# A hybrid decoder layer on one core: first tiles of two feed-forward networks taken block by block, and index scores placed between projection matmuls

## The reference

```python
def _swiglu(x, wg, wu, wd):
    return (jax.nn.silu(x @ wg) * (x @ wu)) @ wd

def _indexer_topk(qi, wi, q_pos, ki, topk):
    s = jnp.einsum('bqhd,bld->bqhl', qi, ki).astype(jnp.float32) * (IDX_DIM ** -0.5)
    score = jnp.einsum('bqhl,bqh->bql', jax.nn.relu(s), wi.astype(jnp.float32)) * (IDX_HEADS ** -0.5)
    ...

def _macaron_layer(x, mixer, f1g, f1u, f1d, ln1g, ln1b, ln2g, ln2b, f2g, f2u, f2d, ln3g, ln3b):
    x = _layernorm(ALPHA * x + 0.5 * _swiglu(x, f1g, f1u, f1d), ln1g, ln1b)
    m, st = mixer(x)
    x = _layernorm(ALPHA * x + m, ln2g, ln2b)
    x = _layernorm(ALPHA * x + 0.5 * _swiglu(x, f2g, f2u, f2d), ln3g, ln3b)
    return x, st
```

## Time and profile before

| | us |
|---|---|
| median of three runs | 1435.36 (1432.1 to 1439.06) |
| the profiled execution | 1438.75 |
| its span in the trace | 1437.1 |
| PE busy | 1372.3 (95% of the span) |
| ACT busy | 451.1 |
| DVE busy | 552.1 |
| POOL busy | 184.6 |

### The profile page before, as it was taken

How to read it: one execution, slowest core, us unless ns; L and a number is a source line. 1 busy time by engine, 2 the same in 40 slices (tenths; PEclk the granted TensorE clock), 3 DMA queues, 4 the chain that set the end, 5 groups by cost and what they waited for, 6 DMA issues and landing times.

```text
span 1437.1 us, 26868 instructions
## 1 busy us (share of the span) xinstructions
PE 1372.3 (95%) x10066; PEld 1201.4 (84%) x10066; DVE 552.1 (38%) x1105; ACT 451.1 (31%) x694; POOL 184.6 (13%) x250
## 2 busy tenths in 40 slices
PE   6999999999999999999999989998899999999994
PEld 6999999999997656777766665567799999999994
DVE  3333233322234236899020444436433333332236
ACT  3343333322233231112231403324533333322234
POOL 0000000033422301222460030003100000000020
PEclk9999999999999989999999978999899999999997
DMA  4222222233322324788757666501132222223231
GB/s 173 88 88 82 80 86 88 84 89 106 106 78 97 120 66 143 260 268 259 265 191 224 222 217 217 191 16 44 44 88 88 88 88 88 88 70 88 88 92 63
DMA packets 69454, 176.78 MB, mean 123 GB/s; under 512 B 9681, under 2 KB 13778, under 8 KB 69138
## 3 DMA queue, kind: packets, MB, share of 16 engines
q1 hardware_dynamic: 59090, 148.09, 32.5%
q0 software_dynamic: 9440, 24.18, 5.1%
q10 hardware_dynamic: 864, 3.73, 0.7%
HBM read 168.93 MB, written 7.02 MB: 122 GB/s over the span
## 4 chain that ended last, share of the span: by engine, by line
PE 93%; DVE 3%; ACT 2%; DMA 1%; issue 1%; ACTq 0%; POOL 0%; DVEq 0%
PE ps L377 91%; PE ps L380 2%; DMA xbuf<-in_x_t 1%; ACT scr L915 1%; DVE scr L1293 1%; DVE rbuf L1286 0%; ACT xbuf L915 0%; ACT x_high L915 0%; DVE rbuf L1298 0%; DVE w_low L1203 0%; ACT big L915 0%; ACT lg L915 0%; ACT w_high L915 0%; DVE big L1286 0%; DVE scr L1276 0%
## 5 line engine op out<-in xcount | busy, mean ns | idle before, releaser
L377 PE MATMUL ps<-x_high,w_high 128*128 128x280 f32 (+1 forms) x1408 | 414.4, 294 | 23.8 <-DVE x_low L1209 10.3
L377 PE MATMUL ps<-x_high,w_low 128*128 128x280 f32 (+1 forms) x1408 | 412.3, 293 | 0.0
L377 PE MATMUL ps<-x_low,w_high 128*128 128x280 f32 (+1 forms) x1408 | 412.1, 293 | 0.0
L1203 DVE TENSOR_TENSOR w_low<-wring,w_high 128x1024 fp32r<-128x1024 f32 (+1 forms) x136 | 166.8, 1228 | 497.2 <-ACT w_high L915 497.1
L377 PEld LDWEIGHTS ps<-x_high,w_high 128*128 128x128 f32 x1408 | 269.2, 191 | 26.6 <-issue 20.0
L915 ACT ACTIVATE w_high<-wring 128x1024 fp32r<-128x1024 f32 (+1 forms) x136 | 140.5, 1034 | 413.1 <-PE ps L377 399.3
L377 PEld LDWEIGHTS ps<-x_low,w_high 128*128 128x128 f32 x1408 | 269.9, 192 | 0.0
L377 PEld LDWEIGHTS ps<-x_high,w_low 128*128 128x128 f32 x1408 | 269.3, 191 | 0.0
L377 PE MATMUL ps<-xbuf,wring 128*128 128x280 f32 x1056 | 263.6, 405 | 5.0 <-ACT xbuf L915 4.1
L377 PEld LDWEIGHTS ps<-xbuf,wring 128*128 128x128 f32 x1056 | 197.5, 191 | 59.6 <-issue 9.1
L377 PE MATMUL ps<-h_high,w_high 128*128 128x280 f32 (+1 forms) x704 | 204.5, 290 | 0.0
(11 more groups left out here) (201 smaller groups left out, 1175.3 us busy)
## 6 DMA issues: line engine op xcount, KB each, us to landing
dring<-in_v_pool SPq DMA_DIRECT2D x128, 256.0 KB, 3.5
wring<-in_wg SPq DMA_DIRECT2D x44, 512.0 KB, 3.5
wring<-in_wu SPq DMA_DIRECT2D x44, 512.0 KB, 3.5
wring<-in_w_in SPq DMA_DIRECT2D x33, 512.0 KB, 4.1
wring<-in_wd SPq DMA_DIRECT2D x32, 512.0 KB, 3.6
dring<-in_k_pool POOLq DMA_DIRECT2D x64, 256.0 KB, 4.4
dring<-in_k_pool SPq DMA_DIRECT2D x64, 256.0 KB, 3.8
wring<-in_wd SPq DMA_DIRECT2D x16, 384.0 KB, 3.1
```

The lines of the kernel that those rows point to most:

```text
L377: return nc.tensor.matmul(out, lhs, rhs, start=start, stop=stop, **kw)
L1203: v.tensor_tensor(wl[:, to, 0:n], w4[:, s, 0:n], wh[:, to, 0:n].bitcast(F32), ALU.subtract) \
```

## The change

**First network.** PE takes tile 0 block by block, both weights and both halves of a block together (12 matmuls), and then `tile(1)` as before. ACT and DVE split up 0 right after the first x block. The constants are issued behind ACT's x splits. SP waits for all four quarters of x before it issues the third and fourth weight tile.

**Second network.** A second pair of buffers (`wh2`, `wl2`, laid over memory that is idle then) takes the splits of gate 1 and up 1, made in the norm: ACT after the fourth square, DVE ahead of the last two adds. PE does half 0 of tiles 0 and 1 together block by block (12 matmuls a block), then half 1 weight by weight. `first_pair` on ACT and DVE handles the hidden values of both tiles and splits the weights of tile 2; the loops of ACT and DVE run one round less.

**Query tiles.** The transposes of the head weights stand between the halves of query tile 0. The scores of queries t stand between the products of query tile t: after each product of the second half for t = 0, after every other product for t = 1 to 3. ACT evicts the tile behind its eight Relus. What `index_queries` and `index_scores` hold was in line before and is unchanged.

```diff
+        w_high2, w_low2 = (over(f"w_{n}2", 2048, h_at + (ZT * T + 2048 * i) * 4) for i, n in enumerate(("high", "low")))
...
                     f, up = divmod(s, 2)
+                    if m == 0 and s == 2:
+                        for q in range(4):
+                            sp.wait_ge(sem(f"xw_in{q}"), 16)
                     weight(s, (wus if up else wgs)[m][f], first=(m == 0))
...
-            def wide_split(m, p, s, high, low, k0=0, kn=KT, total=KT, parts=(0, 1), ready=None, ks=None):
+            def wide_split(m, p, s, high, low, k0=0, kn=KT, total=KT, parts=(0, 1), ks=None, hi=wh, lo=wl):
 
                 for a in parts:
                     for k in ks or range(kn):
-                        if ready is not None:
-                            pe.wait_ge(sem("xl_done"), ready + k + 1)
-                        for j, (w_, x_) in enumerate(((wh, high), (wh, low), (wl, high))):
+                        for j, (w_, x_) in enumerate(((hi, high), (hi, low), (lo, high))):
...
                 pe.wait_ge(sem("h_done"), hdone.up())
-                for a in range(2 if m else 0):
-                    if a == 0:
-                        pe.wait_ge(sem("wl_done"), wl_done.up(2))
+                if m == 0:
                     for k in range(KT):
-                        pe.wait_ge(sem("xl_done"), KT * (1 + a) + k + 1)
+                        pe.wait_ge(sem("xl_done"), k + 1)
                         for up in range(2):
-                            last = wide_split(1, 2 * up, up, xh, xl, parts=(a,), ks=(k,))
-                            if a and k == KT - 1:
+                            if k == 0:
+                                pe.wait_ge(sem("wl_done"), wl_done.up())
+                            last = wide_split(0, 2 * up, up, xh, xl, ks=(k,))
+                            if k == KT - 1:
                                 last.then_inc(sem(f"w_free{up}"), 1)
-                for a in range(0 if m else 2):
-                    for up in range(2):
-                        if a == 0:
-                            pe.wait_ge(sem("wl_done"), wl_done.up())
-                        last = wide_split(m, 2 * up, up, xh, xl, parts=(a,),
-                                          ready=None if up or a > m else KT * (m + a))
-                        if a:
-                            last.then_inc(sem(f"w_free{up}"), 1)
-                tile(1)
+                    tile(1)
+                else:
+                    pe.wait_ge(sem("h_done"), hdone.up())
+                    pe.wait_ge(sem("wl_done"), wl_done.up(4))
+                    split = [dict(), dict(hi=wh2, lo=wl2)]
+                    for k in range(KT):
+                        pe.wait_ge(sem("xl_done"), KT + k + 1)
+                        for j in range(2):
+                            for up in range(2):
+                                wide_split(1, 2 * up + j, up, xh, xl, parts=(0,), ks=(k,), **split[j])
+                    for j in range(2):
+                        for up in range(2):
+                            for k in range(KT):
+                                if j == up == 0:
+                                    pe.wait_ge(sem("xl_done"), 2 * KT + k + 1)
+                                last = wide_split(1, 2 * up + j, up, xh, xl, parts=(1,), ks=(k,), **split[j])
+                            last.then_inc(sem(f"w_free{2 * j + up}"), 1)
...
             first_tile(KW)
 
...
+            def index_queries():
+
+                pe.wait_ge(sem("z_done"), Q)
+                for t in TILES:
+                    tr(ps[:, 6, 64 * t:64 * t + 64], z[64:128, KW, real(t):real(t) + P], 64, 128)
+                mm(ps[:, 7, 0:NS], c("sel")[64:128, :], z[64:128, KW, SMP:T]).then_inc(sem("prep_full"), 1)
+                pe.wait_ge(sem("kid_done"), 2)
+
+            def index_scores(u, t, hd):
+                lo = 64 * (hd % 2)
+                p = u % 2
+                if u >= 2:
+                    pe.wait_ge(sem("rel_done"), u - 1)
+                nk, q = min(SEEN[t], 512), z[lo:lo + 64, QI + hd // 2, real(t):real(t) + P]
+                last = mm(ps[:, 4 + p, 0:nk], q, kid[lo:lo + 64, 0:nk])
+                if t == 3:
+                    pe.wait_ge(sem("rel_done"), u)
+                    last = mm(ps[:, 6, 0:META], q, kid[lo:lo + 64, 512:PL])
+                last.then_inc(sem("s_full"), 1)
 
             u = 0
             for t in TILES:
-                first_tile(Q + t)
+                i = Q + t
+                weight(i % 4)
+                pe.wait_ge(sem("z_done"), i - 1)
                 if t == 3:
                     pe.wait_ge(sem("wi_done"), 1)
...
+                hd = 0
+                for a in range(2):
+                    if t == 0 and a == 1:
+                        index_queries()
+                    for k in range(KT):
+                        last = mm(ps[:, 2 * (i % 2) + a, 0:HALF], w4[:, i % 4, k * P:(k + 1) * P], x[:, k, cols(a)],
+                                  k == 0, k == KT - 1)
+                        if (a == 1 if t == 0 else k % 2 == 0):
+                            index_scores(u, t, hd)
+                            hd, u = hd + 1, u + 1
+                last.then_inc(sem(f"w_free{i % 4}"), 1)
             pe.wait_ge(sem("z_done"), FIRST)
...
-            act.dma_start(cst[:, :], consts).then_inc(sem("cst_in"), 16)
...
+                def first_pair():
+
+                    for j in range(2):
+                        for up in range(2):
+                            w = frees[2 * j + up]
+                            act.wait_ge(w.sem, w.up())
+                        ev(halves(s_buf[:, j, live(m)]), pair(j, m), ACT.Silu).then_inc(sem("s_done"), 1)
+                        act.wait_ge(hdone.sem, hdone.up())
+                        ev(hh[:, j, live(m)], s_buf[:, j, live(m)]).then_inc(sem("hh_done"), 1)
+                        if j == 0:
+                            for up in range(2):
+                                weight_high(up, up)
+
+                if m:
+                    first_pair()
+                with loop(act, FT // 2 - 1 - m, [(w, 1) for w in frees] + [(w, 16) for w in w_in_t] + [(hdone, 2)]) as i:
+                    hidden(i * 2 + 2 * m, 0)
+                    hidden(i * 2 + 2 * m + 1, 1)
...
                     for d in range(KT - 1):
                         square(1, d)
+                        if d == 3:
+                            weight_high(2, 0, out=wh2)
+                            weight_high(3, 1, out=wh2)
...
                 ev(xh[:, k, :], x[:, k, :]).then_inc(sem("xh_done"), 1)
-            weight_high(1, 1)
+                if k == 0:
+                    weight_high(1, 1)
+            act.dma_start(cst[:, :], consts).then_inc(sem("cst_in"), 16)
...
             for t in TILES:
-                first_tile(Q + t)
                 for hd in range(AH):
                     nk = min(SEEN[t], 512)
                     act.wait_ge(sem("s_full"), u + 1)
...
                         last = ev(rel[:, u % 2, 512:PL], ps[:, 6, 0:META], ACT.Relu, scale=AD ** -0.5)
                     last.then_inc(sem("rel_done"), 1)
                     u += 1
+                first_tile(Q + t)
...
+                    if k == 0:
+                        weight_low(1, 1)
...
                     x_lows()
-                    weight_low(1, 1)
...
+                def first_pair():
+
+                    for j in range(2):
+                        dve.wait_ge(sd.sem, sd.up())
+                        v.tensor_tensor(halves(s_buf[:, j, live(m)]), halves(s_buf[:, j, live(m)]), pair(2 + j, m), ALU.mult) \
+                            .then_inc(sem("h_done"), 1)
+                        dve.wait_ge(hd.sem, hd.up())
+                        v.tensor_tensor(hl[:, j, live(m)], s_buf[:, j, live(m)], hh[:, j, live(m)].bitcast(F32), ALU.subtract) \
+                            .then_inc(sem("hl_done"), 1)
+                        if j == 0:
+                            for up in range(2):
+                                weight_low(up, up)
...
             seq(v.scalar_tensor_tensor(halves(r7), pair(2, 1), -KT / CENTRE[1], halves(x[:, KT - 1, live(1)]), ALU.mult, ALU.add))
+            weight_low(2, 0, out=wl2, high=wh2)
+            weight_low(3, 1, out=wl2, high=wh2)
```

More of the change, by code:

```diff
@@ L163, in build @@
         xh, xl, hh, hl = tiles(x_high, KT), tiles(x_low, KT), tiles(h_high, FT), tiles(h_low, FT)
-        wh, wl = (w[:, :].rearrange("p (s n) -> p s n", s=2) for w in (w_high, w_low))
+        wh, wl, wh2, wl2 = (w[:, :].rearrange("p (s n) -> p s n", s=2) for w in (w_high, w_low, w_high2, w_low2))
         w4 = wring[:, :].rearrange("p (s n) -> p s n", s=4)
@@ L529, in _ @@
             first_tile(KW)
-            pe.wait_ge(sem("z_done"), Q)
-            for t in TILES:
-                tr(ps[:, 6, 64 * t:64 * t + 64], z[64:128, KW, real(t):real(t) + P], 64, 128)
-            mm(ps[:, 7, 0:NS], c("sel")[64:128, :], z[64:128, KW, SMP:T]).then_inc(sem("prep_full"), 1)
-            pe.wait_ge(sem("kid_done"), 2)
```

(43 more changed lines are left out.)

## The result

The changed kernel takes 1429.1 us (median) against 1437.1: a ratio of 0.9947, interval 0.9937 to 0.9958, so 7.6 us less, where 16.8 were forecast. The profiled execution went from 1437.1 to 1430.1 us of span; the traces can be laid side by side.

The account below looks back on a forecast made before the run. TensorE holds 93% of the chain of waits, so only its stalls or slow stretches give time: -0.2 - 5.9 - 2.8 - 7.9 = -16.8 us, 1418.6 at the median; own range 1414 to 1423 (64%), wider 1411 to 1426.

Parts of the forecast that it names:

- Start of the first network: First two tiles: earlier dense work and restart, offset by a pause and clock fall; -0.2 us, bounds -2.9 and +0.8.
- Query tiles and index scores: Key tile to sample scores: interleaving removes waits, 54.4 us against 60.3; -5.9 us, bounds -8.7 and -4.8.
- the second rival: Query tiles with scores: each of 64 switches costs a 0.191 us weight load, 12.2 us in all; 1430.8 us, chance 8%.
- the short products: 16-column tails and 144-column scores in the query tiles: weight loads with little to hide behind, 3.1 us taken of 4.2.
- The rule that the prediction did cite: For PE's switches: weight loads overlap matmuls in flight only where row groups differ; would make the second rival the forecast.
- Sample scores: First group of sample scores: dense work before it keeps the clock up; -2.8 us, bounds -2.9 and 0.
- The third rival: Mixed stretch of query tiles and scores runs at half clock, costing 53 us more; about 1472 us, chance 4%.
- Start of the second network: Second feed-forward network, first tiles: waits vanish, -8.4, with first matmul 0.5 late; sum -7.9 us, bounds -9 and -5.
- the rule that the prediction took from the Trainium skill: Splits beside norm sums: a two-SBUF-input VectorE operation and an SBUF-reading GpSimd one exclude each other; term 0.5 us.
- the forecast's 0.5: Second network's first matmul 0.5 us late because splits made ahead share time with GpSimd's sums in the norm.
- the trickle: Second network: PE slowly follows GpSimd's x splits until 1022.85; a clock fall there, 2 us, stood only in a bound.
- its first rival: Clock falls at the sample scores and in the second network's trickle; gain only -12.0 us, 1423.4 us, chance 15%.

Follow-up runs that it names:

- the kernel with full height: Changed kernel with every index score computed over all 128 rows of queries and keys instead of 64; ratio 0.9846 to the kernel before.
- the kernel with the first network's splits ahead: Changed kernel with the first network's second-tile weight splits made ahead and its first pair of tiles ahead of the loop; ratio 0.9920 to before.
- the two kernels with pairs: Changed kernel with index scores two heads at a time, either neighbours (different row halves) or heads of one row half; ratios 0.9827 and 0.9882 to before.
- the one with neighbouring pairs: Changed kernel with scores of two neighbouring heads (different row halves) side by side after every four tile products, two in the first tile; ratio 0.9827 to before.

## Why the prediction was wrong

**Start of the first network: right.** Forecast: the up weight's split at 11.2, the second tile at 27.85, then 1.5 lost to the clock. Measured: 11.37, 28.05, and 400.69 instead of 399.17 for the same 3084 matmuls, which is 1.52. The sum was -0.2 and is 0.0. (The working is 0.1 off: 24.0 and 3.75 make 27.75, not 27.85.)

**Query tiles and index scores: wrong, and this is the error.** The failed step is the one that put the price of a switch aside as the second rival: "Against it: at 488.48, where scores give way to a tile, matmul and weight load start without idle time". The observation was right and its meaning was the opposite. What the rows needed was the load's start beside the matmul's. The weight loads of the kernel before at that place, with the last two of the tile ahead in front:

```profile
483.93 0.42 PEld L377 LDWEIGHTS ps<-xbuf,wring 128*128 128x128 f32 x2
...
488.48 7.37 PEld L377 LDWEIGHTS ps<-xbuf,wring 128*128 128x128 f32 x32
496.22 0.30 PEld L377 LDWEIGHTS ps<-scr,big 64*128 64x128 f32 x4 [0.37 <-issue]
```

The load starts at 488.48, together with the first matmul's row. A hidden load would stand ahead of it, as in the kernel with full height. And from 488.48 to 496.22 there are 7.74 us: 32 x 0.236 + 0.19. So one switch was already inside the tile's 7.81, and dividing 7.81 by 32 spread it over the pace (0.244) instead of showing it. The other argument, that loads of 0.191 hide inside a pace of 0.129, holds in these traces only between operands of the same height.

With that term the sum closes. Of the 54.4 us, tiles lose 1.0 by the true pace and the short products 2.1 (a tail adds about 0.13 to its score, not 0.38), and 64 x 0.191 = 12.2 come on top: 63.5. From the key tile's end, 474.4, to 537.51 it is 63.1. The rest of that part held: PE did not wait for ACT or DVE inside a tile, and at the end of the last tile it waited 0.73 where 1.0 was taken. SP asked for the samples' keys at 539.63, 2.8 us behind its next weight (536.86), and PE did not wait for them.

The Trainium skill had the rule on a page that the prediction did not use: "TensorEngine Tiling (Array Packing)", section Tiling Modes, Key Properties, says that changing the tiling mode drains TensorE, and sets this apart from changing only the tile. The runs here agree with both halves: 0.19 to 0.20 us for each change between 64 and 128 rows, nothing between scores of one height. The rule that the prediction did cite, of "TensorE: Matmul & The Clock Gate" (part 3, the mechanism), is too wide by these runs if it is taken alone (the same section also names a background weight buffer that a load may go to): in the kernel at full height the loads run 0.23 us ahead though all row groups are the same.

**Sample scores: right.** -2.8 forecast, -2.9 measured: the first group takes 3.72 us and not 6.62, at a granted clock of 1.00. PE's row of it in the changed kernel, with the wait for the last tile's eviction in front:

```profile
537.51 3.72 PE L381 MATMUL ps<-lg,spare 128*64 128x512 f32 x20 [0.73 <-ACT big L938]
```

The third rival, half clock through the mixed stretch, did not come: the granted clock was 1.00 in all windows from 476 to 537.

**Start of the second network: right; forecast -7.9, measured -7.0 (-7.5 and the +0.5 ahead of it).** The third tile begins 30.3 us after the first matmul, where 29.5 were forecast, and PE does not stand for its weights. Two terms were off in opposite directions. The splits made ahead did meet GpSimd's (POOL's) sums; DVE and POOL of the changed kernel:

```profile
991.11 4.07 DVE L1246 TENSOR_TENSOR w_low<-wring,w_high 128x1024 fp32r<-128x1024 f32 x2
995.10 0.77 DVE L1686 TENSOR_TENSOR big<-big,ps 128x272 f32<-128x272 f32 x2
```

```profile
988.99 5.11 POOL L1712 TENSOR_TENSOR scr<-scr,acc 128x544 f32<-128x544 f32 x3 [0.15 <-ACT acc L938]
```

Two splits took 4.07 us where 2.46 is their own time, so the trace agrees with the rule that the prediction took from the Trainium skill ("SBUF — State Buffer", the two sides of SBUF) as far as the operations go, and the last add came 1.0 us late. But it did not become a term: the network's first matmul follows the output stretch that starts at 962.01 by 41.61 us, exactly as before the one at 961.54, since PE was still busy with the norm's other sums when the adds came. The 0.5 us by which the first matmul is late arose earlier, between 833 and 861, where nothing was changed; the agreement with the forecast's 0.5 is chance. In the other direction the clock fell in the trickle, which the forecast named as a bound and in its first rival, and did not take. PE waiting for POOL, and the window behind it:

```profile
1020.29 0.39 PE L381 MATMUL ps<-x_high,w_high 128*128 128x272 f32 x1 [0.67 <-POOL x_low L1760]
1021.32 0.39 PE L381 MATMUL ps<-x_high,w_high 128*128 128x272 f32 x1 [0.38 <-POOL x_low L1760]
1022.33 0.60 PE L381 MATMUL ps<-x_high,w_high 128*128 128x272 f32 x1 [0.37 <-POOL x_low L1760]
```

```profile
1022.00:1024.00 2.00, 1.67 (x6) 1.40 (x7) 0.00 (x0) 0.44 (x1) 1.04 (x2) 0.57 0.00 0
```

It costs about 1 us: in the kernel with the first network's splits ahead the same trickle kept a granted clock of 1.00, and from the output stretch to the end of the chain it took 446.67 us, against 447.71 here and 455.19 before. Of the seven traces with this start of the second network the clock stayed at 1.00 in five (446.67 to 447.15 us) and fell in two (447.71 and 448.26). So 7.5 or 8.5 is the gain, depending on that fall, and what decides it is open.

**The sum.** 0.0 + 2.8 - 2.9 + 0.5 - 7.5 = -7.1, the difference of the spans to a tenth. The outcome (1429.1) lies by the second rival (1430.8, given 8%). That rival kept the forecast's prices for the tile's pace and the short products, about 3 us too much, so by its own sum the change would have gained 4.6 us and not 7.6. Its odds were the mistake, and with them the range, which left it out.

## What to carry to other kernels

Interleaving short matmuls into long ones fills waits and keeps the clock, but if the two differ in operand height each change of height costs an exposed weight load, here 0.19 us between 64 and 128 rows. Count these changes before moving anything, and group the short ones (pairs in different row halves were best: half the changes and two scores for the time of one). To see whether the load at a change of operands is hidden, compare the first load of the new group with the group's first matmul: in these traces ahead is hidden (490.21 for 490.44), equal is exposed (494.25 for both), and an idle time of zero on PE says nothing.

## What was not expected of the hardware

Two scores in different row halves overlap completely: per pair the two kernels with pairs differ by 0.45 us at 272 columns, 0.67 at 400 and 1.07 at 512 with the tail, each time one score. The prediction had read a partial overlap from the 0.94 us of four 400-column instructions, which contains an exposed load and a modelled end.

A stretch that no edit touches, from 833.5 to 962 in the changed kernel, takes one of two lengths: 128.0 to 128.6 us in five of the nine traces and 123.8 to 124.3 in the other four. The changed kernel is of the first kind, as the kernel before is; the one with neighbouring pairs is of the second. Windows of the two, in order, at the same work (a row of short matmuls starts at 860.66 in the one, 842.78 in the other):

```profile
860.00:865.00 5.00, 4.34 (x16) 2.51 (x20) 2.08 (x11) 2.60 (x6) 4.07 (x8) 0.69 0.77 281
...
870.00:875.00 5.00, 4.83 (x14) 2.49 (x13) 3.44 (x14) 2.70 (x9) 0.00 (x0) 0.50 0.69 229
```

```profile
844.50:849.50 5.00, 2.43 (x17) 0.94 (x15) 2.66 (x9) 3.67 (x9) 1.69 (x4) 1.00 0.88 322
849.50:854.50 5.00, 4.19 (x16) 2.10 (x16) 4.01 (x17) 2.07 (x7) 0.00 (x0) 0.71 0.53 154
```

In the one the granted clock falls at once behind that row's wait, in the other some 7 us later. That is half of the difference; the other half (27.16 us against 24.79 from the stretch's start to that row) arises ahead of it. What decides it is open. Executions of one kernel differ by as much (1412.3 to 1420.9 us at full height), so it need not be the kernel. It is why spans of different kernels are compared here stage by stage.
